# Products and halvings of the one-token samples on GpSimd, one short sum a group on VectorE; the first gathers of the last stretch asked for inside the last pass

## What is computed

```
proj = x @ w_in                      # z, xbc, dt, uv, gates
y_a  = SSD branch(z, conv(xbc), dt)  # h_t = exp(dt A) h_{t-1} + dt B x^T ;  y = C h
y_b  = u * (W_s LayerNorm(v) + b)    # chunked spatial gating
h    = LN(alpha x + (g_a * (y_a @ w_a) + g_b * (y_b @ w_b)) @ w_out)
out  = LN(alpha h + PEER(h))         # 8 heads x 16 experts: gelu(h . u_e) * gate, times v_e, summed
```

## Time and profile before

| | |
|---|---|
| three runs | median 5419.04 us (5412.84 to 5423.02) |
| the profiled execution | 5414.41 us, of which 5412.4 us are the span |
| TensorE busy | 3615.6 us (67%) |
| VectorE busy | 3404.2 us (63%) |
| GpSimd busy | 2247.4 us (42%) |
| moved | 1672.07 MB, mean 309 GB/s |
| mean granted TensorE clock | 0.827 |

### The profile page before, as it was taken

How to read it: one execution, slowest core, us unless ns; L and a number is a source line. 1 busy time by engine, 2 the same in 40 slices (tenths; PEclk the granted TensorE clock), 3 DMA queues, 4 the chain that set the end, 5 groups by cost and what they waited for, 6 DMA issues and landing times. The chain is left out here.

```text
span 5412.4 us, 43512 instructions
## 1 busy us (share of the span) xinstructions
PE 3615.6 (67%) x16568; PEld 3035.4 (56%) x16568; DVE 3404.2 (63%) x4108; ACT 713.8 (13%) x1568; POOL 2247.4 (42%) x1272
## 2 busy tenths in 40 slices
PE   7989889999999968888878697897940000230000
PEld 5777778888887757677667586786840000000000
DVE  2545441100001859889866664565898999789999
ACT  2233321100000123333311010000100000000000
POOL 1343420100000025555543432443318888778885
PEclk8999999999999989899889898998975555565555
DMA  4565543444443379999999899999749999999998
GB/s 165 192 209 189 206 174 132 144 148 164 164 159 136 126 298 405 421 417 421 411 364 369 358 421 380 389 421 413 311 156 401 420 422 422 422 380 422 421 422 363
DMA packets 278120, 1672.07 MB, mean 309 GB/s; under 512 B 40000, under 2 KB 69248, under 8 KB 84992
## 3 DMA queue, kind: packets, MB, share of 16 engines
q0 software_dynamic: 160640, 1133.71, 51.2%
q1 hardware_dynamic: 117272, 535.57, 26.3%
HBM read 1633.31 MB, written 35.79 MB: 308 GB/s over the span
## 5 line engine op out<-in xcount | busy, mean ns | idle before, releaser
L503 PE MATMUL psum<-rows_a,w_ring 128*128 128x264 f32 x7168 | 1632.1, 389 | 23.2 <-PEq L461 18.9
L342 POOL DMA_INDIRECT rows_a<-in_peer_u,expert x384 | 818.3, 2131 | 1952.7 <-DVE rows_a L398 977.5
L503 PEld LDWEIGHTS psum<-rows_a,w_ring 128*128 128x128 f32 x7168 | 1371.9, 192 | 265.4 <-issue 30.0
L503 PE MATMUL psum<-x_acts,w_ring 128*128 128x256 f32 x5632 | 1260.1, 385 | 129.0 <-PEq L461 60.1
L503 PEld LDWEIGHTS psum<-x_acts,w_ring 128*128 128x128 f32 x5632 | 1086.5, 194 | 287.1 <-issue 81.6
L398 DVE SCALAR_TENSOR_TENSOR rows_a<-rows_a,h_tokens 128x2048 f32<-128x2048 f32 x384 | 878.6, 2289 | 106.6 <-DMA rows_a<-in_peer_u,expert 75.0
L342 POOL DMA_INDIRECT rows_a<-in_peer_v,expert x384 | 591.7, 1541 | 324.8 <-DVE h_tokens L419 159.5
L419 DVE SCALAR_TENSOR_TENSOR h_tokens<-rows_a,coef,h_tokens 128x2048 f32<-128x2048 f32 x256 | 602.5, 2353 | 77.9 <-issue 69.6
L1855 PE MATMUL psum<-acc,selector 8*128 8x512 f32 x64 | 57.5, 1075 | 685.5 <-DVE rows_a L398 478.7
L1855 PEld LDWEIGHTS psum<-acc,selector 8*128 8x128 f32 x64 | 19.9, 326 | 721.7 <-DVE rows_a L398 485.0
L419 DVE SCALAR_TENSOR_TENSOR acc<-rows_a,coef,acc 128x2048 f32<-128x2048 f32 x128 | 300.8, 2350 | 31.2 <-issue 28.1
(11 more groups left out here) (380 smaller groups left out, 2976.7 us busy)
## 6 DMA issues: line engine op xcount, KB each, us to landing
w_ring<-in_w_tiles SPq DMA_DIRECT2D x448, 1024.0 KB, 6.2
rows_a<-in_state_ssm POOLq DMA_DIRECT2D x32, 512.0 KB, 6.6
out_ssm_sample<-rows_a POOLq DMA_DIRECT2D x32, 512.0 KB, 4.2
rows_a<-acum_rows_dram SPq DMA_DIRECT2D x16, 512.0 KB, 6.5
smp_bc<-smp_bc_dram POOLq DMA_DIRECT2D x8, 1024.0 KB, 8.6
branch_b<-acum_rows_dram SPq DMA_DIRECT2D x16, 512.0 KB, 12.3
rows_a<-in_xT SPq DMA_DIRECT2D x3, 2048.0 KB
rows_a<-in_peer_u,expert POOLq DMA_INDIRECT x384, 20.4
```

What stands on the lines that cost most here:

```text
L342: return pool.indirect_dma_start(out=dst, out_offset=None, in_=table, in_offset=bass.IndirectOffsetOnAxis(ap=self.index(s), axis=0))
L503: last = pe.matmul(o, w[:, k * P:(k + 1) * P], x[:, k, :], start=start and k == 0, stop=stop and k == KB - 1)
```

## The change

- `Samples.unit` on GpSimd issues the state's store right behind the add, then multiplies the state by C into `x_b`, and halves the product three times by adding its upper part to its lower (128 to 64 to 32 to 16 columns); the last halving writes into a new buffer `fold` (two groups of four units). The buffer `prods` goes.
- `Samples.sums` on VectorE reduces the 16 columns of a group's four units in one instruction. It stands once a group, behind the product at L1231, for the group before; the last group's stands behind spatial tile 8 in `sgu`.
- The waits of `load` and `load_bc` for `summed` go; one wait for `summed` of two groups before stands ahead of the last halving.
- u and v rows get buffer orders of their own (`ring`). The limit `s < SLOTS` in `rows` goes, so that u rows 260 to 263 are gathered by steps 256 to 259 in the second pass, into the four old buffers. The tail begins with u rows 264 to 267 and v rows 258 to 261, into the new ones.

```diff
@@ Samples.load / load_bc
-            pool.wait_ge(self.summed, r - self.BUFS + 1)
...
-        if GT * g > self.first:
-            pool.wait_ge(self.summed, GT * g - self.first)
@@ Samples.unit
         o(pool.tensor_tensor(s, s, self.xb[:], ALU.add))
+        pool.dma_start(self.target[v], s).then_inc(self.state_out[r % self.BUFS], 16)
+        x = self.xb
+        o(pool.tensor_tensor(x[:], s, self.bc[:, 1], ALU.mult))
+        o(pool.tensor_tensor(x[:, :, 0:64], x[:, :, 0:64], x[:, :, 64:128], ALU.add))
+        o(pool.tensor_tensor(x[:, :, 0:32], x[:, :, 0:32], x[:, :, 32:64], ALU.add))
+        if r >= 2 * GT:
+            pool.wait_ge(self.summed, r // GT - 1)
+        o(pool.tensor_tensor(self.fold[:, r // GT % 2, t], x[:, :, 0:16], x[:, :, 16:32], ALU.add))
         pool.sem_inc(self.ready, 1)
-        pool.dma_start(self.target[v], s).then_inc(self.state_out[r % self.BUFS], 16)
@@ Samples.sums
+    def sums(self, dve, g):
+        r = g - self.first // GT
+        dve.wait_ge(self.ready, GT * (r + 1))
+        dve.tensor_reduce(self.y[:, g], self.fold[:, r % 2], AX_X, ALU.add).then_inc(self.summed, 1)
-        o(dve.tensor_tensor(self.prod[:], self.state[:, r % self.BUFS], self.bc[:, 1], ALU.mult))
-        dve.tensor_reduce(self.y[:, v // GT, v % GT, :], self.prod[:], AX_X, ALU.add).then_inc(self.summed, 1)
@@ Experts
+        self.u_wide, self.v_wide = SLOTS + 8, SLOTS + 8 - lag
+        self.uslot, self.uturn, self.uheld = self.ring(small, big, self.u_wide)
+        self.vslot, self.vturn, self.vheld = self.ring(small, big, self.v_wide)
...
+    def ring(self, small, big, wide):
+        order = list(range(small, big)) + [(wide + j) % small for j in range(small)]
+        slot = [s % small if s < wide else order[(s - wide) % big] for s in range(self.total)]
+        turn = [slot[:s].count(slot[s]) for s in range(self.total)]
+        held = [max((r for r in range(s) if slot[r] == slot[s]), default=-1) for s in range(self.total)]
+        return slot, turn, held
@@ Experts.rows
-        if s < SLOTS:
-            self.u_row(pool, s + 4)
+        self.u_row(pool, s + 4)
@@ ssd, VectorE
                     conv(g, 2)
-                    sum_smp(g - 1, 0)
...
                     conv(g, 3)
-                    sum_smp(g - 1, 1)
...
                     dve.tensor_tensor(flat(yg[:, g % 2]), flat(yg[:, g % 2]), flat(xg), ALU.mult).then_inc(gated, 1)
+                    if ps.smp and g > 0:
+                        smp.sums(dve, g - 1)
@@ sgu, VectorE
-                    if smp and 4 <= m < 4 + GT:
-                        smp.sums(dve, o, GT * (G - 1) + m - 4)
                     if smp and m == 8:
+                        smp.sums(dve, G - 1)
+                        dve.wait_ge(smp.summed, 1)
@@ tail, GpSimd
-                    for s in range(first, first + 4):
-                        ex.u_row(pool, s)
-                    for s in range(first, first + 4):
-                        ex.v_row(pool, s)
+                    for j in range(4):
+                        ex.u_row(pool, ex.u_wide + j)
+                        ex.v_row(pool, ex.v_wide + j)
...
-                    for s in range(SLOTS, ex.total):
+                    for s in range(first, ex.total):
                         ex.u_row(pool, s + 8)
-                        if not first <= s + 8 - ex.lag < first + 4:
-                            ex.v_row(pool, s + 8 - ex.lag)
+                        ex.v_row(pool, s + 8 - ex.lag)
```

More of the change, by code:

```diff
@@ L227, in __init__ @@
         self.root = sb("smp_root", [P, G, NS])
-        self.xb, self.prod = sb("smp_x_b", [P, NS, NST]), sb("smp_prods", [P, NS, NST])
+        self.xb, self.fold = sb("smp_x_b", [P, NS, NST]), sb("smp_folds", [P, 2, GT, NS, NST // 8])
         self.bc = sb("smp_bc", [P, 2, NS, NST])
@@ L275, in stored @@
             pool.wait_ge(self.state_out[j], 16 * ((self.last - j) // self.BUFS + 1))
[L277 to L281, removed]
-        o(dve.tensor_tensor(self.prod[:], self.state[:, r % self.BUFS], self.bc[:, 1], ALU.mult))
-        dve.tensor_reduce(self.y[:, v // GT, v % GT, :], self.prod[:], AX_X, ALU.add).then_inc(self.summed, 1)
-        dve.wait_ge(self.summed, r + 1)
     def gated(self, o, dve, skip):
@@ L311, in __init__ @@
         self.before = SLOTS
-        self.slot = [s % small if s < SLOTS else s % big for s in range(self.total)]
-        self.turn = [self.slot[:s].count(self.slot[s]) for s in range(self.total)]
-        self.held = [max((r for r in range(s) if self.slot[r] == self.slot[s]), default=-1) for s in range(self.total)]
+        self.u_wide, self.v_wide = SLOTS + 8, SLOTS + 8 - lag
+        self.uslot, self.uturn, self.uheld = self.ring(small, big, self.u_wide)
+        self.vslot, self.vturn, self.vheld = self.ring(small, big, self.v_wide)
         self.smp0 = self.items.index(("sample", 0))
@@ L350, in u_row @@
                 pool.wait_ge(self.k.head_done, PH * BLOCK_PASS[b] + j // TOPK + 1)
-            if self.held[s] >= 0:
-                pool.wait_ge(self.dot_done, self.held[s] + 1)
-            self.gather(pool, self.urow[self.slot[s]], self.k.a["peer_u"], s).then_inc(self.u_in[self.slot[s]], 16)
+            if self.uheld[s] >= 0:
+                pool.wait_ge(self.dot_done, self.uheld[s] + 1)
+            self.gather(pool, self.urow[self.uslot[s]], self.k.a["peer_u"], s).then_inc(self.u_in[self.uslot[s]], 16)
     def v_row(self, pool, s):
         if 0 <= s < self.total:
-            if self.held[s] >= 0:
-                self.wait_added(pool, self.held[s])
-            self.gather(pool, self.vrow[self.slot[s]], self.k.a["peer_v"], s).then_inc(self.v_in[self.slot[s]], 16)
+            if self.vheld[s] >= 0:
+                self.wait_added(pool, self.vheld[s])
+            self.gather(pool, self.vrow[self.vslot[s]], self.k.a["peer_v"], s).then_inc(self.v_in[self.vslot[s]], 16)
     def rows(self, pool, s):
-        if s < SLOTS:
-            self.u_row(pool, s + 4)
+        self.u_row(pool, s + 4)
         if s + 4 - self.lag >= 4:
@@ L387, in dot @@
     def dot(self, dve, s):
-        u = self.urow[self.slot[s]]
-        dve.wait_ge(self.u_in[self.slot[s]], 16 * (self.turn[s] + 1))
+        u = self.urow[self.uslot[s]]
+        dve.wait_ge(self.u_in[self.uslot[s]], 16 * (self.uturn[s] + 1))
         if s >= 8:
@@ L415, in add @@
         dve.wait_ge(self.coef_done, q + 1)
-        dve.wait_ge(self.v_in[self.slot[s]], 16 * (self.turn[s] + 1))
+        dve.wait_ge(self.v_in[self.vslot[s]], 16 * (self.vturn[s] + 1))
         if self.added(s) >= 1:
             dve.wait_ge(self.acc_done, self.added(s))
-        dve.scalar_tensor_tensor(out=acc, in0=self.vrow[self.slot[s]], scalar=self.coef[:, s % 8:s % 8 + 1],
+        dve.scalar_tensor_tensor(out=acc, in0=self.vrow[self.vslot[s]], scalar=self.coef[:, s % 8:s % 8 + 1],
                                  in1=acc, op0=ALU.mult, op1=ALU.add).then_inc(self.acc_done, 1)
@@ L1136, in conv @@
                     dve.wait_ge(conv_done, e + 1)
-                def sum_smp(g, t):
-                    if ps.smp and g >= 0:
-                        smp.sums(dve, o, GT * g + t)
                 def spread_chunk(g, q):
@@ L1199, in _ @@
                     conv(g, 3)
-                    sum_smp(g - 1, 1)
                     expert(g, 2)
                     conv(g, 4)
-                    sum_smp(g - 1, 2)
                     expert(g, 3)
                     conv(g, 5)
-                    sum_smp(g - 1, 3)
                     expert(g, 4)
@@ L1860, in _ @@
                         pe.wait_ge(ex.coef_done, s // 4 + 1)
-                        pe.wait_ge(ex.v_in[ex.slot[s]], 16 * (ex.turn[s] + 1))
+                        pe.wait_ge(ex.v_in[ex.vslot[s]], 16 * (ex.vturn[s] + 1))
                         for c in range(4):
                             last = pe.matmul(self.bank[4 + c][0:NS, :], ex.coefm[:, b, :],
-                                             ex.vrow[ex.slot[s]][:, 512 * c:512 * (c + 1)],
+                                             ex.vrow[ex.vslot[s]][:, 512 * c:512 * (c + 1)],
                                              start=(b == 0), stop=(b == NS - 1))
```

## The result

| | before | after |
|---|---|---|
| median | 5417.41 us (4 runs) | 5386.0 us (5380.6 to 5393.87, 4 runs) |
| ratio | | 0.9946, 95% interval 0.993 to 0.9961 |
| profiled execution | 5414.41, span 5412.4 | 5393.87, span 5391.7 |

The change is faster, by 31 us or 0.54%. The forecast was 5356 us, 63 us less than the 5419.04 us known then: the sign and the range (5338 to 5394) held, the size did not, since only half of the forecast gain came. The time lies where rival B had put it (5372 to 5395). The profiled execution is the longest of the four, so the gain of 20.7 us that the two spans show is smaller than that of the medians.

What follows compares the result with a forecast made beforehand. TensorE's waits at `chunk_a` for SiLU delayed by VectorE and GpSimd bound the first pass, gathers the tail. 5414.41 - 53 (61.4 less 8) - 10 = 5351 us profiled, 5356 as median; range 5338 to 5394.

Steps and rivals of the forecast that it cites:

- rival B: First pass: contention takes most of the gain back, TensorE waiting at `rms` instead of `chunk_a`; 5372 to 5395 us; chance 0.27.
- The waits that go: First pass: TensorE's waits at `chunk_a` vanish whole in seven of eight groups, period 88.35 to 79.94 us.
- the 61.4 us at most: First pass: upper limit of the gain, 58.9 us from seven periods without waits plus 2.5 behind group 7's wait.
- GpSimd's prices: GpSimd's samples units: product 2.34 to 2.40 us, halvings 1.27, 0.74 and 0.47; a unit 14.2 us, a group 67.
- Rival D: First pass: GpSimd becomes the bound and the kernel slower, 5549 us if the new operations were three times as dear; chance 0.04.
- What contention gives back: First pass, chain ahead of `rms`: VectorE held up by GpSimd costs 8 us, between 0 and 48, leaving 53 us net.
- The price of a meeting: Chain ahead of `rms` meeting GpSimd: late by 3.7 us plus two stalls of 1.2; with slow clock 6.9 us a group.
- the 48 us end: First pass: upper bound of contention's cost, every VectorE instruction with two SBUF inputs waiting beside GpSimd, in seven groups.
- The gathers: Second pass's end and tail: four u rows gathered early leave 518 rows instead of 522; gain 10 us, bounds 0 and 12.
- the head start: Tail: VectorE starts some 9 us earlier, its idle time at the first dot about 11 us instead of 21.
- Both signs of being wrong: Forecast wrong if TensorE's period stays above 84 us, or the tail from its first gather is not 10 us shorter.
- `sgu`: Last group's units move into the projections of v in `sgu`: nothing gained, nothing lost, no wait added.

Runs made afterwards that it cites:

- rms_later: The whole change, with `rms(g - 1)` behind projection 2 instead of projection 1 in TensorE's first-pass list: 5356.29 us, ratio 0.9892 to the kernel before.
- gathers_sel_late: Kernel before plus only the gathers' part, with the tail's two memsets and two selects moved to step 330: 5410.17 us, ratio 0.9986 to before.
- gathers_quiet: Kernel before plus only the gathers' part, with just u rows 260 and 261 asked for inside the pass: 5412.23 us, ratio 0.9987 to before.

## Why the prediction was wrong

**The waits that go: right.** The wait at `chunk_a` was to vanish and did. A period without waits was to be 79.94 us and is 79.80, and the 61.4 us at most are 62.8 in `rms_later`: the slow clock behind each wait, read as 2.5 us from two windows, belonged into the sum.

**GpSimd's prices: right but for the halvings.** Product 2364 ns on average against 2.34 to 2.40 forecast; the halvings 1447, 830 and 469 ns against 1.27, 0.74 and 0.47, with waits for VectorE in them:

```profile
L267 POOL TENSOR_TENSOR smp_x_b<-rows_a,smp_bc 128x1024 f32<-128x1024 f32 x28 | 66.2, 2364 | 0.6
...
L268 POOL TENSOR_TENSOR smp_x_b<-smp_x_b 128x512 f32<-128x512 f32 x28 | 40.5, 1447 | 2.2
...
L269 POOL TENSOR_TENSOR smp_x_b<-smp_x_b 128x256 f32<-128x256 f32 x28 | 23.2, 830 | 2.2
L272 POOL TENSOR_TENSOR smp_folds<-smp_x_b 128x128 f32<-128x128 f32 x28 | 13.1, 469 | 2.2
```

Rival D (GpSimd as the bound) was far off: 57 us busy in a group of 80.

**What contention gives back: the step that failed.** It was put at 8 us between bounds of 0 and 48; it was 36.5 (693.4 - 656.9), of which 24.3 are waits and the rest mostly work at the lower clock behind them. Place and mechanism were those of rival B: the chain to L1231 gets late by conv of tile 0 and the next instructions, and the cover of 1.9 us is gone at once. The price of a meeting was right too (3.7 us plus two stalls of 1.2 forecast, 4.4 to 6.9 us measured); what was wrong is how often they meet, five groups of seven instead of about one. The value was taken from L1156, whose median was the bare 172 ns. That was the wrong row: it is one short copy, while the chain has five longer instructions with two SBUF inputs in series (three of conv, L1171, L1232), so even a fair chance at each gives a late chain. And its median came from a schedule in which GpSimd stood idle for much of the time, which the change was to end. The near row was the earlier trace rows, the same conv held up for 3.7 us; taking it for granted in most groups gives 5 or 6 of seven times 6.9, 34 to 41 us, and a time of 5382 to 5389. B had 0.27 and deserved the larger part.

The Trainium skill (SBUF — State Buffer, "SBUF: two separate sides") has the rule that a VectorE instruction with two SBUF inputs waits for GpSimd's whole instruction; the prediction put the time by it at the 48 us end. The trace agrees: L1134 takes 6.08 us beside L1177 at 1.12, and the waits came in five groups of seven.

**The gathers: 10 us forecast, 2 measured; two terms were missing.** The transfers saved were right (9.9 us once nothing else was in the way). But the gathers under way at the pass's end hold GpSimd at the barrier: the first gather of the tail came 4.3 us later behind the last dot, and VectorE's idle time ahead of the tail's first dot fell from 21 to 14.8 us, not to 11. The prediction looked for room in the transfers and for instructions queued behind the four gathers, and did not ask what else waits for a gather; the 10.55 us of idleness ahead of the first gather, with two rows under way, was there to be read. And the head start was to come from VectorE being busy 9 us earlier; that very work slows GpSimd's issues from one in 1.24 us to one in 2.2 to 3, so eight gathers no longer fill the queue over the 5 us of selects. That took 4.5 us. The cost of the selects is shown by `gathers_sel_late`; that VectorE's work is what slows the issues is read from the traces, where the two go together, and no run took that work away.

**The signs that were named.** Both signs of being wrong came: TensorE's period from `chunk_a(0, 0)` to `chunk_a(7, 0)` is 85.0 us on average (limit 84), and the tail from its first gather is 5.9 us shorter, not 10. `chunk_a(7, 0)` starts at 704.5 us instead of about 675. GpSimd's units follow each other every 15.2 to 16.0 us in group 0, as forecast.

**`sgu`: right.** 267.2 us against 267.3. The rest of the passes is unchanged but for the second pass's `sgu`, which takes 329.1 us after and 324.3 before in these two executions. It takes 323 to 331 us in the others too, and 330.3 us in `gathers_quiet` as well as 324.0 us in `rms_later`, so no part of the change explains it; that scatter is left open.

## What to carry to other kernels

When a wait is removed, list every chain with little cover in the same period, and price each with the worst row of the kind that it will meet, not with a median from a schedule in which the other engine stood idle. Work moved to GpSimd is not free beside VectorE: look where VectorE's instructions with two SBUF inputs stand in series ahead of something TensorE needs, and give that point a projection more of cover; here one line in TensorE's list was worth 30 us. Before a barrier, don't start gathers that won't have landed well before the slowest engine gets there; here the last 5 us behind their bytes counted too.

## What the runs showed of the hardware

- GpSimd's DRAIN at the end of the stage ended 4.5 to 4.9 us after the last bytes of its gathers had moved, with two, four or no rows asked for near the end, and the barrier behind it waited. With two rows of 1 MB asked for near the end the first gather behind it came 16.3 to 16.4 us after the start of the last dot, with four 19.8 to 20.6, with none 6.7.
- The issue of a gather on GpSimd took 0.94 us with VectorE idle and mostly 1.9 to 2.8 with VectorE at its dots and adds (2048 columns, two SBUF inputs). Beside VectorE's searches in the choice of experts it took 0.94 too (4005.78 and 4013.16 us after the change). The first eight of the tail before, beside an idle VectorE, took 0.94 us each:

```profile
4066.34 0.94 POOL L342 DMA_INDIRECT rows_b<-in_peer_u,expert  x1 [0.30 <-issue]
4067.58 0.94 POOL L342 DMA_INDIRECT rows_b<-in_peer_u,expert  x1 [0.30 <-issue]
```

- A wait of 4 to 7 us of TensorE cost 2.2 to 2.5 us more in work at the lower clock behind it: 82.31 us of busy time (granted clock 0.96) against 80.04 in the next group (1.00) after the change, and 82.43 against 79.94 before, for the same instructions.
